# Three of four modulation chunks summed off TensorE, in the opening of a one-core diffusion block

## The chip, the cores and the metric

The kernel is one program on one core of a Trainium2 chip. The metric is device time in microseconds (us). A core has TensorE (PE: matmuls; weight loads are listed as PEld), VectorE (DVE), ScalarE (ACT), GpSimd (POOL) and SyncE (SP, whose queue issues almost all DMAs). They run side by side and wait for each other on semaphores. A matmul writes PSUM, which has eight banks of 512 fp32 columns; everything else lies in SBUF.

## The reference

One layer of a transformer block over 512 latent tokens and 256 context tokens of width 1024, in fp32. What matters here is how it begins:

```
mod_lat = silu(c) @ w_ada + b_ada          # w_ada: 1024 x 6144; shift, scale, gate, twice
mod_ctx = silu(c_ctx) @ w_ada + b_ada
h  = rmsnorm(x,   norm1_g) * (1 + sc1)  + sh1      # latent tokens
hc = rmsnorm(ctx, norm1_g) * (1 + csc1) + csh1     # context tokens
p  = h @ w_in                                       # all columns
pc = hc @ w_in[:, :288]                             # the keys' columns alone
```

Behind it come the latent attention, a short convolution, a gated merge, a gated MLP and the final norm. They hold nine tenths of the time and are not touched.

## The kernel before

Every fp32 matrix product is done as three matmuls: each operand is split into a rounded high part and the low rest, and `mm3` (L420 to L424) adds hi*hi, lo*hi and hi*lo in PSUM. So each weight tile and each activation tile needs two element-wise steps: a copy that rounds (usually ACT) and a subtraction for the low part (DVE or POOL).

The opening makes `h` transposed, feature tile by feature tile (eight tiles `k` of 128 features), and multiplies each with its rows of `w_in` as it comes. Feature tiles are handled in four chunks `c_` of two. For tile k it needs shift and scale, which are columns of `mod_lat` and `mod_ctx`. Of `w_ada` only the 2 x 1024 columns for `sh1` and `sc1` are read here. A chunk is 256 columns of each, times 1024 rows, and comes as four slots of `adaraw` (`ada_load`, L474), each with two row blocks of 128 x 512.

The chunks are summed over the 1024 rows in two ways:

- Chunk 0. For the tokens, DVE accumulates `adaraw * silu(c)` over eight row blocks into PSUM bank 3 and at the end into `first_x` (`first_token`, L1101). For the context, ACT scales the same eight blocks into `parts` (`context_scale`, L788), and POOL adds the eight (`first_context_add`, L611). What is left is a sum over 128 partitions: PE multiplies with a column of ones (`first_sums` L1589; for the context the last four matmuls of `late_columns` L1606), and the result stands as columns, one element per partition. DVE adds the bias (`first_mods` L1132, `first_mods_context` L1140).
- Chunks 1 to 3. The weights are split (ACT `ada_hi` L760, DVE `ada_lo` L1162, one 128 x 1024 tile per slot). PE multiplies them with `chl`, which holds silu(c) and silu(c_ctx) in two parts, 16 matmuls for a chunk (`mod_sums`, L1576), tokens and context at once. ACT copies the four rows out of PSUM (`mod_rows1`, L764), PE turns them into columns (`mod_columns`, L1621), DVE adds the bias (`mods1`, L1166).

With shift and scale for tile k there, ACT computes the high part of `h` (`stream_hi` L778), DVE the value and the low part (`stream_value` L1176, `stream_lo` L1186). PE then does `latents(k)` (L1628): 15 matmuls of 512 columns with the tile of `w_in` that ACT and POOL have split (`latent_hi` L770, `latent_lo` L604). The same helpers with n = 8 to 15 make the context's tiles `chi` and `clo`, after all four chunks.

Before this, four tiles of x are loaded, squared (`token_rms` L745), transposed on PE (`token_columns` L1554) and scaled by their inverse rms, which PE spreads over partitions (`spread_rinv` L1599), ACT copies (`rinv_copy` L755) and DVE applies (`scale_low`, `scale_up`). Two tiles of ctx follow in chunks 1 and 2 (`token_norm` L1155, `lower_copy` L1150, `upper_copy` L740).

After the chunks, PE projects the rotary key (24 matmuls of 512 columns, L1673 to L1678). Then comes the context loop (72 matmuls of 256 columns, L1683 to L1694), which first waits for `cq_lo`: DVE's low part of the query latent (L1246), which stands in DVE's program behind all eight context tiles. The queries and keys follow.

The order of work on each engine is the order in which its block is written. DVE's opening is L1194 to L1242, ACT's L793 to L850, POOL's L618 to L628, PE's L1641 to L1694, SP's L497 to L514. An `ada_load` of the first twelve waits, for its slot, until the earlier user has read it.

Of the kernel before, what the change touches and what calls it, by code (L numbers as in the profile page):

```python
# [26 lines left out]
P = 128  # L27
D = 1024
T = 512
# [42 lines left out]
U_KR = U_ADA + 2 * DT - 4  # L72
# [25 lines left out]
def build(nc, x, c, ctx, c_ctx, w_ada, b_ada, norm1_g, w_in, q_norm_g, kv_norm_g, w_uq, w_ukv, conv_w,  # L98
# [3 lines left out]
    with stack:  # L102
# [8 lines left out]
        whi = sb("whi", [P, SLOTS, UNIT], F32R)  # L111
        wlo = sb("wlo", [P, SLOTS, UNIT], F32R)
# [29 lines left out]
        sb("gap0", [P, 768], scope=early)  # L142
# [148 lines left out]
        def arrived(e, u, slot):  # L291
            r = slot % RAW
            if isinstance(u, int) and u < U_KR:
                e.wait_ge(ada_loaded[slot], 32 * (u // SLOTS + 2))
            else:
                e.wait_ge(raw_loaded[r], 32 * ((u - r - U_KR) // RAW + 1) if isinstance(u, int) else (u - r - U_KR) * 16 + 32)
# [115 lines left out]
        def context_part(k):  # L412

            return parts[:, k, :]
# [36 lines left out]
        def _(sp):  # L451
# [143 lines left out]
        def _(pool):  # L595
# [15 lines left out]
            def first_context_add(k):  # L611

                pool.wait_ge(s("ctx_part"), k + 1)
                wait(pool, s("first_ctx"), k - 1)
                nc.gpsimd.tensor_tensor(out=first_ctx, in0=context_part(0) if k == 1 else first_ctx, in1=context_part(k),
                                        op=ALU.add).then_inc(s("first_ctx"), 1)
# [105 lines left out]
        def _(act):  # L722
# [41 lines left out]
            def mod_rows1(c_):  # L764

                used(act, 4 * c_ - 1)
                wait(act, s("cols1_ps"), c_ + 1)
# [10 lines left out]
            def stream_hi(n):  # L778
# [3 lines left out]
                if n >= DT and k < 2:  # L782
                    act.wait_ge(s("mods1_ctx"), 4)
# [4 lines left out]
            def context_scale(k):  # L788

                act.wait_ge(ada_loaded[k // 2], 32)  # L790
                nc.scalar.activation(context_part(k), first_part(k), ACT.Copy, scale=cvec[:, k, 1:2]).then_inc(s("ctx_part"), 1)
# [3 lines left out]
            token_rms(0)  # L795
            rinv_copy(0)
            context_scale(2)
            context_scale(3)
            token_rms(1)
            rinv_copy(1)  # L800
            token_rms(2)
            rinv_copy(2)
            token_rms(3)
            latent_hi(0)
            rinv_copy(3)
            context_scale(4)
            context_scale(5)
            stream_hi(0)
            stream_hi(1)
            context_scale(6)  # L810
            context_scale(7)
            latent_hi(1)
            for c_ in range(1, CHUNKS):
                for u in range(4 * c_ - 4, 4 * c_):
                    ada_hi(u)
                mod_rows1(c_)
# [278 lines left out]
        def _(dve):  # L1095
# [5 lines left out]
            def first_token(k):  # L1101

                dve.wait_ge(ada_loaded[k // 2], 32)
                if k == 0:
                    nc.vector.tensor_scalar(ps[:, 3, :], first_part(k), cvec[:, k, 0:1], None, ALU.mult).then_inc(s("first_x"), 1)
                else:
                    dve.wait_ge(s("first_x"), k)
# [32 lines left out]
            def first_mods_context():  # L1140

                dve.wait_ge(s("prm_ps"), 2)
                for j in range(2):
                    at = CTX_SUM_AT + j
                    nc.vector.tensor_scalar(shift[:, 1:2, j], ps[:, 7, at:at + 1], prm[:, R_BADA + j:R_BADA + j + 1], None,
                                            ALU.add).then_inc(s("mods1_ctx"), 1)
                    nc.vector.tensor_scalar(gain[:, 1:2, j], ps[:, 7, at + 2:at + 3], prm[:, R_N1 + j:R_N1 + j + 1],
                                            gain0[:, j:j + 1], ALU.mult, ALU.add).then_inc(s("mods1_ctx"), 1)
# [13 lines left out]
            def ada_lo(u):  # L1162

                split_lo(dve, u, u % SLOTS, nc.vector)
# [10 lines left out]

            def stream_value(n):  # L1176
# [3 lines left out]
                if n >= DT and k < 2:  # L1180
                    dve.wait_ge(s("mods1_ctx"), 4)
# [4 lines left out]
            def stream_lo(n):  # L1186
# [37 lines left out]
            for c_ in range(1, CHUNKS):  # L1224
                for u in range(4 * c_ - 4, 4 * c_):
                    ada_lo(u)
                if c_ == 2:
# [3 lines left out]
                    first_mods_context()  # L1231
                mods1(c_)
# [308 lines left out]
        def _(pe):  # L1541
# [34 lines left out]
            def mod_sums(u):  # L1576

                c_, n = u // 4 + 1, u % 4
                unit(u)
                if n == 0:  # L1580
                    wait(pe, s("rows1"), c_ - 1)
                    pe.wait_ge(s("mods1"), 4 * c_)
# [6 lines left out]
            def first_sums(j):  # L1589
# [7 lines left out]
                last.then_inc(s("cols1_ps"), 1)  # L1597

# [22 lines left out]
            def mod_columns(c_):  # L1621

                pe.wait_ge(s("rows1"), c_)
# [431 lines left out]
```

## Time and profile before

| what | value |
|---|---|
| three timed runs | 840.03, 840.4, 841.66 us; median 840.4 |
| the profiled execution | 841.12 us, of it a span of 839.1 us |
| PE busy | 811.4 us (97% of the span) |
| DVE, ACT, POOL busy | 467.1, 373.6, 381.2 us |
| TensorE's granted clock, mean | 0.989 of full speed |

Times below are microseconds from the start of the span. A row of the timeline gives the start, the busy time, the engine, the line, the operation, output and inputs, how many instructions were merged, and in brackets how long the engine had been idle and what ended that. Matmuls overlap: one of 512 columns is listed with 0.39 us although the next one starts 0.23 us later.

### The profile page before, as it was taken

How to read it: one execution, taken by the hardware profiler on the slowest of the kernel's cores; microseconds unless marked ns; L12 is line 12 of the kernel's file. 1: busy time of each engine (PE TensorE's matmuls, PEld its weight loads, DVE VectorE, ACT ScalarE, POOL GpSimd, SP SyncE). 2: the span in 40 equal slices, each digit the busy share in tenths (PEclk: the TensorE clock that was granted, in tenths of full speed). 3: DMA queues.
4: the chain of work that ended last, by engine and by line, in shares of the span. 5: the costliest groups of instructions: out<-in, count | busy, mean ns of one | idle time of the engine just before them, and what ended most of it. 6: DMA issues, size and time to landing. Idle time of an engine off the chain costs nothing.

```text
span 839.1 us, 11438 instructions
## 1 busy us (share of the span) xinstructions
PE 811.4 (97%) x3937; PEld 676.4 (81%) x3937; DVE 467.1 (56%) x635; ACT 373.6 (45%) x592; POOL 381.2 (45%) x197
## 2 busy tenths in 40 slices
PE   4799999999999999999999999999999999999996
PEld 4578977888888888888788988888888888888884
DVE  4787596788888467877303565555555555000005
ACT  6566456666667322322423664334444433221125
POOL 2623494436442554555544054444444444443434
PEclk9899999999999999999899999999999999999998
DMA  8661242111110688777273033333333332322212
GB/s 288 208 193 48 54 113 64 33 44 52 26 51 27 212 261 267 237 231 221 78 249 101 1 101 116 87 97 100 100 100 100 91 93 92 100 101 100 85 42 101
DMA packets 120289, 97.82 MB, mean 117 GB/s; under 512 B 13660, under 2 KB 106105, under 8 KB 120249
## 3 DMA queue, kind: packets, MB, share of 16 engines
q1 hardware_dynamic: 120137, 97.26, 37.9%
q8 instruction: 25, 0.41, 0.2%
q14 instruction: 15, 0.12, 0.1%
q10 hardware_dynamic: 112, 0.04, 0.0%
HBM read 95.17 MB, written 2.10 MB: 116 GB/s over the span
## 4 chain that ended last, share of the span: by engine, by line
PE 89%; DVE 5%; ACT 3%; POOL 1%; issue 1%; DMA 1%; SPq 0%; POOLq 0%; DVEq 0%; ACTq 0%
PE ps L422 25%; PE ps L424 24%; PE ps L423 24%; PE ps L1725 7%; PE ps L1832 3%; PE ps L1821 2%; DVE wlo L341 1%; PE ps L1585 1%; DMA adaraw<-w_ada_dram 1%; POOL wlo L341 1%; ACT work L749 1%; PE ps L1899 0%; PE ps L1917 0%; DVE x L1520 0%; ACT work L1073 0%
## 5 line engine op out<-in xcount | busy, mean ns | idle before, releaser
L341 POOL TENSOR_TENSOR wlo<-raw,whi 128x1024 fp32r<-128x1024 f32 (+4 forms) x125 | 281.2, 2257 | 363.7 <-ACT whi L333 363.2
L422 PE MATMUL ps<-hhi,whi 128*128 128x512 f32 (+1 forms) x520 | 196.2, 377 | 0.2 <-DVE hlo L1467 0.2
L424 PE MATMUL ps<-hhi,wlo 128*128 128x512 f32 (+1 forms) x520 | 195.8, 377 | 0.0
L423 PE MATMUL ps<-hlo,whi 128*128 128x512 f32 (+1 forms) x520 | 195.7, 376 | 0.0
L333 ACT ACTIVATE whi<-raw 128x1024 fp32r<-128x1024 f32 (+4 forms) x125 | 118.2, 957 | 132.4 <-PE ps L424 77.5
L424 PEld LDWEIGHTS ps<-hhi,wlo 128*128 128x128 f32 x520 | 97.9, 188 | 18.1
L422 PEld LDWEIGHTS ps<-hhi,whi 128*128 128x128 f32 x520 | 97.9, 188 | 18.1 <-DVE hlo L1467 0.4
L423 PEld LDWEIGHTS ps<-hlo,whi 128*128 128x128 f32 x520 | 97.9, 188 | 17.8
L1495 DVE SCALAR_TENSOR_TENSOR work<-ps,prm,work 128x511 f32<-128x511 f32 x44 | 33.0, 750 | 75.0 <-ACT work L1049 74.0
L1400 DVE SCALAR_TENSOR_TENSOR adacc<-ada,cvec,adacc 128x1024 f32<-128x1024 f32 x28 | 60.7, 2204 | 18.5 <-DMA ada<-w_ada_dram 18.4
L422 PE MATMUL ps<-whi,fhi 128*128 128x512 f32 x176 | 69.8, 396 | 0.0
L423 PE MATMUL ps<-wlo,fhi 128*128 128x512 f32 x176 | 69.7, 396 | 0.0
L424 PE MATMUL ps<-whi,flo 128*128 128x512 f32 x176 | 69.7, 396 | 0.0
L1049 ACT ACTIVATE work<-ps,prm 128x512 f32<-128x512 f32 x44 | 34.2, 778 | 72.2 <-PE ps L424 72.1
L1518 DVE TENSOR_TENSOR ps<-ps,gbc 128x512 f32<-128x512 f32 x8 | 5.5, 688 | 102.9 <-PE ps L424 102.9
L1504 DVE TENSOR_TENSOR work<-work 128x512 f32<-128x512 f32 x22 | 44.2, 2010 | 6.2 <-DVE work L1498 3.8
L1725 PE MATMUL ps<-hhi,whi 128*128 128x512 f32 x96 | 38.8, 404 | 2.1 <-POOL wlo L341 2.1
L1346 DVE TENSOR_REDUCE ps<-ps 128x1 f32<-128x768 f32 x32 | 30.9, 965 | 17.0 <-PE ps L424 16.7
L422 PEld LDWEIGHTS ps<-whi,fhi 128*128 128x128 f32 x176 | 33.1, 188 | 8.3 <-DVE work L1498 0.4
L424 PEld LDWEIGHTS ps<-whi,flo 128*128 128x128 f32 x176 | 33.1, 188 | 8.0
L423 PEld LDWEIGHTS ps<-wlo,fhi 128*128 128x128 f32 x176 | 33.1, 188 | 7.9
L1056 ACT ACTIVATE fhi<-work 128x512 f32 (+1 forms) x22 | 13.9, 633 | 57.1 <-DVE work L1504 57.1
(290 smaller groups left out, 1533.2 us busy)
## 6 DMA issues: line engine op xcount, KB each, us to landing
raw<-w_up_dram SPq DMA_DIRECT2D x88, 256.0 KB, 3.2
ada<-w_ada_dram SPq DMA_DIRECT2D x32, 512.0 KB, 6.3
raw<-w_in_dram SPq DMA_DIRECT2D x56, 256.0 KB, 4.3
raw<-w_down_dram SPq DMA_DIRECT2D x44, 256.0 KB, 2.7
adaraw<-w_ada_dram SPq DMA_DIRECT2D x32, 256.0 KB, 4.8
raw<-w_o_dram SPq DMA_DIRECT2D x16, 256.0 KB, 3.1
xt<-x_dram SPq DMA_DIRECT2D x4, 512.0 KB, 7.3
raw<-w_attn_out_dram SPq DMA_DIRECT2D x8, 256.0 KB, 2.8
```

What stands on the lines that cost most here:

```text
L333: ins = nc.scalar.activation(h, r, ACT.Copy)
L341: ins = (engine or nc.gpsimd).tensor_tensor(out=l, in0=r, in1=h.bitcast(F32), op=ALU.subtract)
L422: pe.matmul(o, l[0], r[0], start=start, stop=False)
L423: pe.matmul(o, l[0], r[1], start=False, stop=False)
L424: return pe.matmul(o, l[1], r[0], start=False, stop=stop)
L1049: nc.scalar.activation(work[:, 3 * jj + n, :], ps[:, (4 if first else 0) + 2 * jj + n, :], ACT.Identity, bias=col(prm, R_FB + n * FT + j), ...
L1346: nc.vector.reduce_max(top, wide(2 * (turn(g) % 2)), AX.X, negate=True).then_inc(s("nmax"), 1)
L1400: nc.vector.scalar_tensor_tensor(out=adacc[:, gg:gg + D], in0=ada2[:, n % 3, :], scalar=cvec[:, k, 0:1], in1=adacc[:, gg:gg + D], op0=ALU. ...
L1495: nc.vector.scalar_tensor_tensor(out=u[:, 1:T], in0=p[:, 0:T - 1], scalar=col(prm, R_FW + n * FT + j), in1=u[:, 1:T], op0=ALU.mult, op1=AL ...
L1504: nc.vector.tensor_tensor(out=work[:, 3 * jj + 2, :], in0=work[:, 3 * jj, :], in1=work[:, 3 * jj + 1, :], op=ALU.mult).then_inc(s("f_prod" ...
L1725: last = pe.matmul(ps[:, 7, :], tile_of(wlo if term == 2 else whi, u % SLOTS, k), (hlo if term == 1 else hhi)[:, k, :], start=i == 0, stop ...
L1832: last = pe.matmul(ps[:, 6, q], vs[:, kt, h, :], p_[:, kt, q], start=kt == 0 and n == 0, stop=kt == KT - 1 and n == 1)
```

## The change

Chunks 1 and 2 are now summed as chunk 0 is; chunk 3 alone still goes through the split weights. So `mod_sums` runs once instead of three times, and `U_KR`, the number of weight units before the rotary key's, goes from 12 to 4.

- DVE does `first_token(k, c_)` for eight blocks in chunks 1 and 2, ACT `context_scale(k, c_)`, POOL `context_add(c_, k)`. Chunk 1's scaled blocks go to `parts1`, which lies where `wlo` lies; chunk 2's reuse `parts`, which lies where `chi` and `clo` lie.
- PE does `vector_sums(c_)` for the tokens in the chunk, and `context_sums()` for both context chunks once, after all eight `latents`. DVE's `mods_context(1)` and `(2)` follow it. All eight context tiles on ACT and DVE, and PE's context loop, now wait for all twelve context values (`mods1_ctx` at 12), where before only the first two tiles waited for four.
- In the token phase ACT scales two context blocks between one x tile's squares and its `rinv_copy`, and copies the last tile's before `latent_hi(0)`. DVE takes `token_rinv(0)` before `first_token(2)`.
- POOL does all seven adds of chunk 0 before `latent_lo(0)`; chunk 1's seven stand behind `latent_lo(3)`, chunk 2's behind `latent_lo(5)`.

```diff
-U_KR = U_ADA + 2 * DT - 4
+U_KR = U_ADA + SLOTS
+VECTOR_CHUNKS = 3
...
@@ SP, ada_load: every slot waits for both readers
-                    if u < SLOTS:
-                        sp.wait_ge(s("first_x"), 2 * u + 2)
-                        sp.wait_ge(s("ctx_part"), 2 * u + 2)
-                    else:
-                        sp.wait_ge(w_lo, u - SLOTS + 1)
+                    sp.wait_ge(s("first_x"), 2 * u + 2)
+                    sp.wait_ge(s("ctx_part"), 2 * u + 2)
...
@@ POOL
-            for k in range(1, 4):
-                first_context_add(k)
+            for k in range(1, DT):
+                context_add(0, k)
             latent_lo(0)
             latent_lo(1)
-            for k in range(4, DT):
-                first_context_add(k)
-            for k in range(2, DT):
-                latent_lo(k)
+            for c_ in (1, 2):
+                latent_lo(2 * c_)
+                latent_lo(2 * c_ + 1)
+                for k in range(1, DT):
+                    context_add(c_, k)
+            latent_lo(DT - 2)
+            latent_lo(DT - 1)
...
@@ ACT
+            for t in range(TT):
+                token_rms(t)
+                if t < TT - 1:
+                    context_scale(2 * t + 2)
+                    context_scale(2 * t + 3)
+                rinv_copy(t)
             latent_hi(0)
-            rinv_copy(3)
-            context_scale(4)
-            context_scale(5)
             stream_hi(0)
             stream_hi(1)
-            context_scale(6)
-            context_scale(7)
             latent_hi(1)
             for c_ in range(1, CHUNKS):
-                for u in range(4 * c_ - 4, 4 * c_):
-                    ada_hi(u)
-                mod_rows1(c_)
+                if c_ < VECTOR_CHUNKS:
+                    for k in range(DT):
+                        context_scale(k, c_)
+                else:
+                    for u in range(SLOTS):
+                        ada_hi(u)
+                    mod_rows1()
...
@@ ACT stream_hi and DVE stream_value
-                if n >= DT and k < 2:
-                    act.wait_ge(s("mods1_ctx"), 4)
+                if n >= DT:
+                    act.wait_ge(s("mods1_ctx"), 12)
...
@@ DVE
+            token_rinv(0)
             first_token(2)
             first_token(3)
-            token_rinv(0)
...
             for c_ in range(1, CHUNKS):
-                for u in range(4 * c_ - 4, 4 * c_):
-                    ada_lo(u)
+                if c_ < VECTOR_CHUNKS:
+                    for k in range(DT):
+                        first_token(k, c_)
+                else:
+                    for u in range(SLOTS):
+                        ada_lo(u)
...
+            for c_ in (1, 2):
+                mods_context(c_)
             for n in range(DT, 2 * DT):
                 stream_value(n)
                 stream_lo(n)
...
@@ PE
+            def vector_sums(c_):
+                pe.wait_ge(s("first_x"), DT * (c_ + 1))
+                pe.wait_ge(s("mods1"), 4 * c_)
+                for m in range(4):
+                    last = pe.matmul(ps[:, 3, m:m + 1], first_x[:, m * P:(m + 1) * P], ones[:, 0:1], start=True, stop=True)
+                last.then_inc(s("cols1_ps"), 1)
+
+            def context_sums():
+                pe.wait_ge(s("first_ctx"), VECTOR_CHUNKS * (DT - 1))
+                pe.wait_ge(s("xT_low"), KT)
+                for c_ in (1, 2):
+                    for m in range(4):
+                        last = pe.matmul(ps[:, 5, 4 * c_ + m:4 * c_ + m + 1], context_sum(c_)[:, m * P:(m + 1) * P], ones[:, 0:1],
+                                         start=True, stop=True)
+                last.then_inc(s("prm_ps"), 1)
...
                 if c_ + 1 < CHUNKS:
-                    for u in range(4 * c_, 4 * c_ + 4):
-                        mod_sums(u)
-                    latents(2 * c_ + 1, (0,) if c_ else (2,))
-                    mod_columns(c_ + 1)
-                    latents(2 * c_ + 1, (1, 2, 3, 4) if c_ else (3, 4))
+                    if c_ + 1 < VECTOR_CHUNKS:
+                        vector_sums(c_ + 1)
+                        latents(2 * c_ + 1, every if c_ else (2, 3, 4))
+                    else:
+                        for u in range(SLOTS):
+                            mod_sums(u)
+                        latents(2 * c_ + 1, (0,))
+                        mod_columns()
+                        latents(2 * c_ + 1, (1, 2, 3, 4))
...
             pe.wait_ge(s("mods1"), 2 * DT)
+            context_sums()
             for n in range(2):
                 u = U_KR + n
                 unit(u)
...
             pe.wait_ge(s("cq_lo"), 1)
+            pe.wait_ge(s("mods1_ctx"), 12)
             for k in range(DT):
```

## Rows read from the trace of the kernel before

**Rows 1.** The page: busy time, share of the span, instructions of each engine.

```profile
PE 811.4 (97%) x3937; PEld 676.4 (81%) x3937; DVE 467.1 (56%) x635; ACT 373.6 (45%) x592; POOL 381.2 (45%) x197
```

**Rows 2.** Waits between 20 and 80 us: total, times, longest.

```profile
PE ps L1585 <- DVE wlo L341: 2.7, 3, 1.0
```

**Rows 3.** Timeline of the token phase: first_token (DVE), rinv_copy (ACT).

```profile
9.05 1.61 DVE L1108 SCALAR_TENSOR_TENSOR ps<-adaraw,cvec,ps 128x512 f32<-128x512 f32 x2 [1.69 <-DMA adaraw<-w_ada_dram]
...
14.59 1.61 DVE L1108 SCALAR_TENSOR_TENSOR ps<-adaraw,cvec,ps 128x512 f32<-128x512 f32 x2
...
11.62 0.28 ACT L758 ACTIVATE work<-ps 128x128 f32<-128x128 f32 x1 [2.50 <-PE ps L1603]
```

**Rows 4.** Timeline of PE, from the first latents to the context loop.

```profile
23.88 0.77 PE L422 MATMUL ps<-hhi,lqhi 128*128 128x512 f32 x1 [0.95 <-DVE hlo L1191]
...
46.01 1.05 PE L1618 MATMUL ps<-ones,work 128*128 128x1 f32 x8
...
55.46 1.04 PE L1572 MATMUL ps<-ident,xt 128*128 128x128 f32 x8
...
65.20 0.40 PE L422 MATMUL ps<-hhi,lqhi 128*128 128x512 f32 x1
...
77.57 0.40 PE L424 MATMUL ps<-hhi,lklo 128*128 128x512 f32 x1
...
83.28 0.28 PE L422 MATMUL ps<-chi,lkhi 128*128 128x256 f32 x1
```

**Rows 5.** Timeline of DVE: splits, modulation columns, context tiles, low query part.

```profile
27.81 8.62 DVE L341 TENSOR_TENSOR wlo<-adaraw,whi 128x1024 fp32r<-128x1024 f32 x4 [0.93 <-ACT whi L333]
39.44 0.22 DVE L1171 TENSOR_SCALAR shift<-ps,prm 128x2 f32<-128x2 f32 x1 [3.01 <-PE ps L1625]
...
40.08 1.00 DVE L1183 TENSOR_SCALAR ht<-xnT,gain,shift 128x512 f32<-128x512 f32 x1
...
44.89 4.62 DVE L341 TENSOR_TENSOR wlo<-adaraw,whi 128x1024 fp32r<-128x1024 f32 x4
...
59.48 4.63 DVE L341 TENSOR_TENSOR wlo<-adaraw,whi 128x1024 fp32r<-128x1024 f32 x4
...
75.51 0.77 DVE L1191 TENSOR_TENSOR clo<-ht,chi 128x256 fp32r<-128x256 f32 x1 [1.90 <-ACT chi L785]
...
81.70 1.40 DVE L1246 SCALAR_TENSOR_TENSOR cqlo<-ps,prm,cqhi 128x512 fp32r<-128x512 f32 x2
```

**Rows 6.** Timeline of POOL: adds of context parts.

```profile
12.58 2.68 POOL L615 TENSOR_TENSOR work<-work,parts 128x512 f32<-128x512 f32 x2 [3.89 <-ACT parts L791]
...
28.58 8.99 POOL L615 TENSOR_TENSOR work<-work,parts 128x512 f32<-128x512 f32 x4
```

**Rows 7.** Groups by shape, 0 to 100 us: busy, mean ns, idle before.

```profile
L608 POOL TENSOR_TENSOR lqlo<-raw,lqhi 128x384 fp32r<-128x384 f32 x8 | 8.6, 1081 | 0.0
```

**Rows 8.** Timeline of ACT: context parts, square of a ctx tile, first context tiles.

```profile
24.80 1.32 ACT L791 ACTIVATE parts<-adaraw,cvec 128x512 f32<-128x512 f32 x2
...
57.03 1.05 ACT L749 ACTIVATE work<-xt 128x1024 f32<-128x1024 f32 x1
...
74.82 2.07 ACT L785 ACTIVATE chi<-xnT,shift,gain 128x256 fp32r<-128x256 f32 x4
```

**Rows 9.** Windows: from:to, length, busy (instructions) per engine, granted clock, DMA share, GB/s.

```profile
22.00:22.50 0.50, 0.36 (x3) 0.36 (x3) 0.46 (x2) 0.50 (x2) 0.41 (x1) 0.92 0.00 0
...
24.00:28.00 4.00, 4.00 (x10) 3.13 (x11) 2.67 (x6) 3.92 (x7) 1.09 (x2) 0.50 0.43 137
...
29.00:29.50 0.50, 0.50 (x3) 0.36 (x3) 0.50 (x1) 0.50 (x1) 0.50 (x1) 0.75 0.87 231
...
112.00:116.00 4.00, 1.91 (x9) 1.26 (x8) 3.84 (x6) 3.31 (x6) 3.86 (x3) 1.00 0.43 89
...
832.00:835.00 3.00, 0.00 (x0) 0.00 (x0) 2.76 (x5) 1.85 (x6) 3.00 (x2) 0.97 0.04 14
```

More of the change, by code:

```diff
@@ L410, in first_part, with context_part, context_sum @@
             return adaraw[:, k // 2, k % 2 * T:(k % 2 + 1) * T]
-        def context_part(k):
-            return parts[:, k, :]
+        def context_part(c_, k):
+            return (parts1 if c_ == 1 else parts)[:, k, :]
+        def context_sum(c_):
+            return (first_ctx, ctx1[:], parts[:, 0, :])[c_]
         def tile_of(t, slot, k, n=P):
@@ L609, in latent_lo, with context_add @@
                 ins.then_inc(s("win_lo"), 1)
[L611 to L616, printed above, removed]
-            for k in range(1, 4):
-                first_context_add(k)
+            def context_add(c_, k):
+                pool.wait_ge(s("ctx_part"), DT * c_ + k + 1)
+                wait(pool, s("first_ctx"), (DT - 1) * c_ + k - 1)
+                nc.gpsimd.tensor_tensor(out=context_sum(c_), in0=context_part(c_, 0) if k == 1 else context_sum(c_),
+                                        in1=context_part(c_, k), op=ALU.add).then_inc(s("first_ctx"), 1)
+            for k in range(1, DT):
+                context_add(0, k)
             latent_lo(0)
             latent_lo(1)
-            for k in range(4, DT):
-                first_context_add(k)
-            for k in range(2, DT):
-                latent_lo(k)
+            for c_ in (1, 2):
[5 more added lines that the diff above has]
+            latent_lo(DT - 1)
             pool.wait_ge(w_lo, U_KR)
@@ L762, in ada_hi, with mod_rows1 @@
                 split_hi(act, u, u % SLOTS)
-            def mod_rows1(c_):
-                used(act, 4 * c_ - 1)
-                wait(act, s("cols1_ps"), c_ + 1)
+            def mod_rows1():
+                used(act, SLOTS - 1)
+                act.wait_ge(s("cols1_ps"), CHUNKS)
                 nc.scalar.activation(rows1[:], ps[0:4, 3, :], ACT.Copy).then_inc(s("rows1"), 1)
@@ L1174, in mods1, with vector_mods @@
                                             gain0[:, k:k + 1], ALU.mult, ALU.add).then_inc(s("mods1"), 1)
+            def vector_mods(c_):
+                dve.wait_ge(s("cols1_ps"), c_ + 2)
+                for j in range(2):
+                    k = 2 * c_ + j
+                    nc.vector.tensor_scalar(shift[:, 0:1, k], ps[:, 3, j:j + 1], prm[:, R_BADA + k:R_BADA + k + 1], None,
+                                            ALU.add).then_inc(s("mods1"), 1)
+                    nc.vector.tensor_scalar(gain[:, 0:1, k], ps[:, 3, 2 + j:3 + j], prm[:, R_N1 + k:R_N1 + k + 1],
+                                            gain0[:, k:k + 1], ALU.mult, ALU.add).then_inc(s("mods1"), 1)
             def stream_value(n):
@@ L1179, in stream_value @@
                 dve.wait_ge(s("mods1"), 2 * k + 2)
-                if n >= DT and k < 2:
-                    dve.wait_ge(s("mods1_ctx"), 4)
+                if n >= DT:
+                    dve.wait_ge(s("mods1_ctx"), 12)
                 dve.wait_ge(s("xT_low" if k < 4 else "xT_up"), TT if n < DT else KT)
@@ L1576, in mod_sums @@
             def mod_sums(u):
-                c_, n = u // 4 + 1, u % 4
+                n = u
                 unit(u)
                 if n == 0:
-                    wait(pe, s("rows1"), c_ - 1)
-                    pe.wait_ge(s("mods1"), 4 * c_)
+                    pe.wait_ge(s("mods1"), 4 * VECTOR_CHUNKS)
                 for i in range(2):
@@ L1619, in late_columns, with mod_columns @@
                 last.then_inc(s("prm_ps"), 1)
-            def mod_columns(c_):
-                pe.wait_ge(s("rows1"), c_)
+            def mod_columns():
+                pe.wait_ge(s("rows1"), 1)
                 for m in range(4):
```

53 lines of the change are left out of this document (28 added, 25 removed).

## The prediction, on record before the changed kernel ran

> **What bounds the kernel now.** I read the page first: PE is busy 811.4 us of 839.1 [rows 1], so the whole is PE-bound and only a stretch where PE waits can give time without removing matmuls. The waits of the opening come next. From 20 to 80 us PE waited for DVE's weight splits three times, 2.7 us in all [rows 2]. The other cost of the sums through weights is PE's own work. Then the timelines, engine by engine, because the change rewrites four programs and each of its waits has to be placed. Three times matter on PE: the latents start at 23.88, the last `mod_sums` is over at 65.20, the last latents at 77.81 (77.57 + 0.24); and the context loop starts at 83.28 [rows 4]. What follows the context loop is untouched and hangs on it: ACT's and DVE's statistics read the loop's banks, and they feed the queries. So I price the change by how far the loop's start moves.
>
> **What is taken from PE.** 32 of 48 `mod_sums` matmuls. A matmul of 512 columns comes every 0.23 us (24 from 77.81 to 83.28 [rows 4]): 32 x 0.23 = 7.4 us. `vector_sums` costs what `mod_columns` did, about 1.0 us (the four column sums of `late_columns` take 1.05 [rows 4]). `context_sums` adds eight, 2.0 us. PE's own work falls by 5.4 us. Whether that arrives depends on the waits, and I now walk through them.
>
> **Token phase: 1.6 us earlier.** `token_rinv(0)` stood behind two `first_token` that waited 1.69 for a DMA until 9.05 and ran 1.61; so ACT sat idle 2.50 until 11.62 [rows 3]. Now the first inverse is ready near 9.3, and ACT fills the gap with two context parts (1.32 a pair [rows 8]). Tile 1's squares start near 10.7 instead of 13.0; from there the x tiles' DMAs and the alternation of the engines take part of it back. I take 1.6 for the first latents, 23.88 to 22.3; below, 0.5 (DMA-bound); above, 2.3.
>
> **Chunk 1.** DVE was free for it at 26.9 (27.81 less 0.93 [rows 5]), now at 25.3. Two dependent `first_token` take 1.61, so one each 0.86 [rows 3]; eight take 6.9, to 32.2. ACT's eight parts (0.61 each) and the loads, which now follow earlier readers, are done before. PE has 21 matmuls in hand, 7.4 us as before (half of them at half clock), until 29.7, and waits 2.5. Sums 1.0, columns on DVE 0.64 (39.44 to 40.08 [rows 5]): 33.9, against 40.1. Here the change is 6 us ahead.
>
> **Chunk 2.** From the columns' arrival to the next chunk DVE took 5.45 (39.44 to 44.89 [rows 5]); 0.45 of it was a 1.00 us `stream_value` that met POOL, and POOL's `latent_lo(2)` is now over by then. So 33.2 + 5.0 = 38.2, plus 6.9 = 45.1. PE meanwhile: nine matmuls, 15 of `latents(2)`, 1.5 of `late_columns`: done at 40.5. Then it stands at `vector_sums(2)` for 4.6 us, although `latents(3)`, written behind it, is ready at 37. The sums end at 46.1.
>
> **Chunk 3.** `latents(3)` takes 3.5 at full clock, until 49.6. But the clock fell at 22.4 after three microseconds with little on PE, and rose again at 29.2 [rows 9]; at half clock ten matmuls took 4.0 us where ten take 2.3. Under load that lasted 5.3 us (23.88 to 29.2), 13 matmuls with 0.18 more each. After a silence of 4.6 I expect a fall, and these 2.4 more: 52.0. ACT and DVE then need the ctx tile: from PE's transposes (55.46 [rows 4]) to ACT's squares (57.03 [rows 8]) to the first split (59.48 [rows 5]) it took 4.0. Splits start at 53.6, or 56.0 with the fall.
> Beside them runs POOL. One add alone takes 1.34, and 2.25 beside DVE's splits, which then take 2.15 instead of 1.15 (8.62 for four against 4.63) [rows 5, 6]. `latent_lo(3)` ends near 37.1 (1.08 for its larger half [rows 7], 1.7 for both), chunk 1's adds at 46.5, `latent_lo(4)` and `(5)`, which wait for their high parts, at 50.9, and chunk 2's seven would end at 60.3 alone. From 53.6 all four splits meet adds: 8.6, to 62.2. From 56.0 three do: 3 x 2.15 + 1.15 = 7.6, to 63.6. The last four `mod_sums` end 1.1 later: 63.3, or 64.7 with the fall, against 65.20. So nearly all of the six microseconds is given back: the removed matmuls had stood where the others now wait.
> [...]
>
> **The end: 5.3 us later.** From the last `mod_sums` PE is solid: 12.6 us to the end of the latents (65.20 to 77.81). That puts it at 75.9 to 77.3. Before, the context tiles were made while PE was in the last latents (ACT from 74.82 [rows 8]), and `cqlo` began at 81.70 [rows 5], in time for 83.28. Now nothing of the context starts until: `context_sums` 2.0; eight columns on DVE 1.3 and a handover 0.15; ACT's first tile 0.6 (of 2.07 for four); DVE's eight tiles 6.0 (75.51 to 81.70 was 6.2 with one slow); `cqlo` 0.75. Sum 10.8 after the latents, where the loop started after 5.5. The rotary key's matmuls hide 5.5 of it; 3.4 is a new PE silence. If DVE's part overlapped perfectly with the sums the least is 9.5; with POOL's splits in the way 11.8.
>
> **Sum.** Loop start 75.9 + 10.8 = 86.7 without a fall in chunk 3, 77.3 + 10.8 = 88.1 with it: +3.4 or +4.8. After the 3.4 us silence a second fall may slow the loop's 72 matmuls: nothing to 2.4; a silent gap of 2.1 at 112 to 116 left the clock at 1.00, and the silence at the end of the kernel shows the fall between 832 and 835 [rows 9]. I take half, 1.2. Forecast +6.0: 847.1 for an execution like the profiled one (841.12: span 839.1 and 2.0 around it), and 846.4 against the median of 840.4.
>
> **The rivals.**
> A, no fall of the clock: +3.4, 843.8. For it: the gap of 2.1 without one. Against it: 4.6 is more than double.
> B, more loss: both falls in full and one more in the 2.5 us wait of chunk 1, or a DMA behind one of the new waits (an `ada_load` now waits for ACT's and DVE's reading): +8 to +9, 849.
> C, faster: the splits of chunk 3 run alone, 4.6 instead of 8.6. It decides at one point, whether POOL has finished chunk 2's adds when DVE starts to split (53.6 without a fall). Then `mod_sums` ends at 59.3, latents at 71.9, loop at 82.7; with `first_token` at its busy 0.75 instead of 0.86, 1.8 less again: -2.4, 838.0. Against it: 21 adds and six latent pairs are 38 us of POOL even alone, and chunk 1's start only after `latent_lo(3)`.
> D, no change: the token phase gives 2.3, the splits meet two adds and not four, and no fall: 3.4 - 0.7 - 2.0 = +0.7, 841.1.
>
> **How the numbers follow.** Forecast 0.50, A 0.22, B 0.12, D 0.08, C 0.08. The range 842.3 to 849.6 leaves out C, D and the far edge of B. A difference under 0.2% (1.7 us) can't be told from none: slower 0.85, same 0.08, faster 0.07.
>
> **What would show it.** PE's first latents near 22.3; PE idle before `vector_sums(1)` by 2.5 and before `vector_sums(2)` by 4 to 5, with a granted clock of half behind it; four splits of DVE in 7 to 9 us beside POOL's adds; the last latents ending 0.5 to 2 earlier than 77.81; then an idle PE before the context loop, with `cqlo` as what ends it, and the loop near 87 to 88. I am wrong if the loop starts before 84, if PE doesn't wait there, or if the time behind the loop doesn't shift with it.

## The result: 850.6 us, slower by 1.1%

| what | before | after |
|---|---|---|
| median of the timed runs | 840.4 us (838.87 to 841.66, 5 runs) | 850.61 us (850.01 to 850.98, 5 runs) |
| the profiled execution, its span | 841.12, 839.1 | 850.98, 849.2 |
| context loop starts | 83.28 | 92.46 |
| mean granted clock | 0.989 | 0.977 |

The ratio is 1.0114 [1.0103, 1.0125]. The forecast was 846.4, its range 842.3 to 849.6: the direction was right, the size fell a microsecond outside the range. 9.2 us of the loss stand at the start of the context loop, the rest behind it. The page after, busy time of each engine:

```profile
PE 811.5 (96%) x3921; PEld 676.1 (80%) x3921; DVE 475.9 (56%) x651; ACT 374.4 (44%) x598; POOL 399.2 (47%) x211
```

PE is as busy as before [rows 1], although 32 matmuls of `mod_sums` are gone: the eight of `context_sums` are new, and more of the rest run at half clock and take longer (mean granted clock 0.977, before 0.989). The waits of PE between 20 and 110 us (who waited <- for what, us in total, times, longest):

```profile
PE ps L1632 <- DVE work L1116: 7.3, 2, 3.7
PE ps L431 <- DVE clo L1211: 3.7, 1, 3.7
PE ps L1613 <- DVE wlo L346: 3.5, 4, 1.8
```

Before there were three waits on `wlo`, 2.7 us in all [rows 2]. Now the two column sums wait 7.3, the context loop 3.7, and the one chunk of splits that is left 3.5, more than the three did. PE's timeline after, in the same columns as [rows 4]:

```profile
22.74 0.77 PE L431 MATMUL ps<-hhi,lqhi 128*128 128x512 f32 x1 [1.17 <-DVE hlo L1211]
...
32.90 1.86 PE L1632 MATMUL ps<-ones,work 128*128 128x1 f32 x8 [3.63 <-DVE work L1116]
34.62 0.77 PE L431 MATMUL ps<-hhi,lqhi 128*128 128x512 f32 x1
...
47.71 1.86 PE L1632 MATMUL ps<-ones,work 128*128 128x1 f32 x8 [3.69 <-DVE work L1116]
49.43 0.77 PE L431 MATMUL ps<-hhi,lqhi 128*128 128x512 f32 x1
...
54.68 1.03 PE L1601 MATMUL ps<-ident,xt 128*128 128x128 f32 x8
...
68.47 0.40 PE L1613 MATMUL ps<-wlo,chl 128*128 128x512 f32 x1
...
81.30 0.95 PE L1641 MATMUL ps<-ones,ctx 128*128 128x1 f32 x8
82.11 1.03 PE L1641 MATMUL ps<-ones,parts 128*128 128x1 f32 x8
...
92.46 0.36 PE L431 MATMUL ps<-chi,lkhi 128*128 128x256 f32 x1 [3.71 <-DVE clo L1211]
```

Both groups of column sums come after a silence of 3.6 to 3.7 us and take 1.86 where four sums took 1.05 before [rows 4]. The granted clock in those stretches (stretch, length, PE busy, PEclk, DMA share, GB/s):

```profile
26.00:29.00 3.00, 3.00 (x14) 1.00 0.54 152
33.00:36.00 3.00, 3.00 (x11) 0.50 0.99 313
36.00:39.00 3.00, 3.00 (x8) 0.50 0.60 204
48.00:50.00 2.00, 2.00 (x9) 0.50 0.90 304
50.00:53.00 3.00, 3.00 (x9) 0.50 0.66 197
64.00:66.00 2.00, 1.80 (x4) 0.50 0.01 4
108.00:109.00 1.00, 1.00 (x4) 0.50 0.89 236
```

0.50 is 1.2 GHz, 1.00 is 2.4 GHz. Between 26 and 110 us the clock is down four times: from the end of each wait for the column sums into the matmuls behind them, in the middle of the last splits, and once behind the loop. DVE's timeline after shows how its stages went:

```profile
26.51 2.47 DVE L1116 SCALAR_TENSOR_TENSOR ps<-adaraw,cvec,ps 128x512 f32<-128x512 f32 x3
...
32.10 0.75 DVE L1116 SCALAR_TENSOR_TENSOR work<-adaraw,cvec,ps 128x512 f32<-128x512 f32 x1
34.80 0.22 DVE L1191 TENSOR_SCALAR shift<-ps,prm 128x1 f32<-128x1 f32 x1 [1.96 <-PE ps L1632]
35.43 0.54 DVE L1203 TENSOR_SCALAR ht<-xnT,gain,shift 128x512 f32<-128x512 f32 x1
36.76 1.10 DVE L1203 TENSOR_SCALAR ht<-xnT,gain,shift 128x512 f32<-128x512 f32 x1
37.90 1.38 DVE L1211 TENSOR_TENSOR hlo<-ht,hhi 128x512 fp32r<-128x512 f32 x1
39.39 1.59 DVE L1168 TENSOR_SCALAR xt<-xt,small 128x1024 f32<-128x1024 f32 x1
40.91 0.74 DVE L1113 TENSOR_SCALAR ps<-adaraw,cvec 128x512 f32<-128x512 f32 x1
41.75 5.05 DVE L1116 SCALAR_TENSOR_TENSOR ps<-adaraw,cvec,ps 128x512 f32<-128x512 f32 x6
...
57.95 0.77 DVE L1168 TENSOR_SCALAR xt<-xt,small 128x1024 f32<-128x1024 f32 x1
58.77 8.84 DVE L346 TENSOR_TENSOR wlo<-adaraw,whi 128x1024 fp32r<-128x1024 f32 x4
```

And POOL's:

```profile
38.70 1.74 POOL L621 TENSOR_TENSOR ctx<-parts 128x512 f32<-128x512 f32 x1
40.58 8.61 POOL L621 TENSOR_TENSOR ctx<-ctx,parts 128x512 f32<-128x512 f32 x6
...
53.55 10.75 POOL L621 TENSOR_TENSOR parts<-parts 128x512 f32<-128x512 f32 x6
64.80 1.72 POOL L621 TENSOR_TENSOR parts<-parts 128x512 f32<-128x512 f32 x1 [0.50 <-POOL parts L621]
```

The four splits begin at 58.77 and take 8.84, to 67.61; the adds run until 66.52, so that each split meets them. `mod_sums` ends at 68.70, where before it was 65.20.

### The profile page after: what moved, and what is told of

It is laid out like the page before. It is cut to its first block, busy times and chain, and to the rows that moved or that the text cites. A ratio compares the mean times of both kernels' runs of the same rounds, so it can differ in the third digit from the quotient of the medians.

```text
span 849.2 us, 11477 instructions
## 1 busy us (share of the span) xinstructions
PE 811.5 (96%) x3921; PEld 676.1 (80%) x3921; DVE 475.9 (56%) x651; ACT 374.4 (44%) x598; POOL 399.2 (47%) x211
## 4 chain that ended last, share of the span: by engine, by line
PE 83%; DVE 2%; ACT 2%; issue 2%; POOL 1%; DMA 1%; POOLq 0%; SPq 0%; ACTq 0%; DVEq 0%
PE ps L431 23%; PE ps L433 23%; PE ps L432 23%; PE ps L1777 7%; PE ps L1884 3%; PE ps L1873 2%; DMA raw<-w_ukv_dram 1%; PE ps L1951 0%; PE ps L1969 0%; DVE x L1549 0%; ACT work L1080 0%; PE ps L1920 0%; DVE ps L1547 0%; ACT whi L338 0%; ACT chi L794 0%
## 5 line engine op out<-in xcount | busy, mean ns | idle before, releaser
L1429 DVE SCALAR_TENSOR_TENSOR adacc<-ada,cvec,adacc 128x1024 f32<-128x1024 f32 x28 | 65.5, 2381 | 13.3 <-DMA ada<-w_ada_dram 13.3
L1777 PE MATMUL ps<-hlo,whi 128*128 128x512 f32 x96 | 38.5, 401 | 0.0
```

The source lines that it names most:

```text
L1429: nc.vector.scalar_tensor_tensor(out=adacc[:, gg:gg + D], in0=ada2[:, n % 3, :], scalar=cvec[:, k, 0:1], in1=adacc[:, gg:gg + D], op0=ALU. ...
L1777: last = pe.matmul(ps[:, 7, :], tile_of(wlo if term == 2 else whi, u % SLOTS, k), (hlo if term == 1 else hhi)[:, k, :], start=i == 0, stop ...
```

## The experiments

There were seventeen runs, each beside runs of the kernel before. Its medians in the five sets were 842.06, 841.8, 841.45, 841.62 and 841.69. Some kernels issue matmuls that nothing needs, into a bank that is free there, to keep PE busy; four (adds_short, short_filled, short_filled_early and short_early) leave out chunk 2's context sum but for 8 of its 512 columns. "Loop" is the start of the context loop in the profile.

| kernel | us | ratio to before [95%] | loop |
|---|---|---|---|
| tail_alone | 847.38 | 1.0069 [1.0047, 1.0091] | 87.50 |
| tail_filled | 844.51 | 1.0036 [1.0023, 1.0049] | 87.58 |
| ctx_early | 845.38 | 1.0045 [1.0031, 1.0059] | 88.86 |
| adds_short | 846.17 | 1.0060 [1.0039, 1.0080] | 88.13 |
| adds_later | 846.54 | 1.0062 [1.0040, 1.0084] | 89.35 |
| token_alone | 835.29 | 0.9933 [0.9907, 0.9958] | 78.19 |
| token_again | 835.30 | 0.9919 [0.9904, 0.9934] | 79.08 |
| token_warm | 836.52 | 0.9927 [0.9899, 0.9955] | 79.01 |
| after_again | 852.04 | 1.0127 [1.0095, 1.0159] | 92.30 |
| latents_first | 848.67 | 1.0084 [1.0052, 1.0116] | 88.24 |
| filler | 850.90 | 1.0107 [1.0075, 1.0139] | 92.56 |
| both_filled | 847.21 | 1.0072 [1.0049, 1.0095] | 89.41 |
| early_and_first | 845.84 | 1.0042 [1.0021, 1.0063] | 89.24 |
| all_filled | 842.42 | 1.0002 [0.9988, 1.0016] | 84.62 |
| short_filled | 842.61 | 1.0006 [0.9997, 1.0016] | 85.08 |
| short_filled_early | 841.68 | 0.9999 [0.9990, 1.0009] | 83.85 |
| short_early | 838.84 | 0.9959 [0.9945, 0.9973] | 81.25 |

**The tail.** The kernel before, with nothing of the change but the context's sums and tiles behind the last latents; and the changed kernel with the sums ahead of `latents(7)`.

```diff
 # tail_alone, on the kernel before: late_columns no longer sums first_ctx
+            context_sums()          # PE: its four columns, behind latents(7)
 ...
-                    first_mods_context()
+            first_mods_context()    # DVE: behind all latent tiles
 # ctx_early, on the changed kernel
                 else:
+                    context_sums()
                     latents(2 * c_ + 1, every)
```

> The kernel before, with one thing of the change: the four column sums of the context's chunk 0, and the eight context tiles that need them, come only behind the last latents, instead of beside the second chunk. Tail theory (the new wait of the context loop is a serial chain): sums 1.0, four columns on DVE 0.75, then 7.85 as in the changed kernel from its last column (84.6) to the loop (92.46), 9.6 behind the last latents instead of 5.5, so the loop starts 4.1 later at 87.4 and the whole takes 844.5. Rival (the context tiles are hidden by the rotary key's matmuls and the loss sits in the chunks): within 1 us of the kernel before, 840.4 to 841.4. Rival (clock: a silence of over 3 us on PE lets the clock fall in the loop): 2 more, 846.5.

> The changed kernel, with the eight column sums of the context placed before the last latents instead of behind them; nothing else. Tail theory: the sums end at 79.7 instead of 83.1, the chain of 9.3 behind them is the same, so the loop starts at 89.1 instead of 92.5 and the whole is 3.4 shorter, 847.2. Rival (the loop is held by something else than this chain, the rotary key's matmuls or POOL's splits): under 1 us shorter, 849.6 to 850.6.

The loop started where it was expected both times: 87.50 in tail_alone and 88.86 in ctx_early. The tail by itself costs 4.2 us at the loop; the early sums give back 3.6 of it in the changed kernel. The wholes missed in both directions. ctx_early came out 1.8 under its 847.2, with executions spread from 843.36 to 848.83; the profiled one is the slowest of the ten. tail_alone came out 2.9 over its 844.5; the kernel before was 1.7 higher in this set too, and the rest shows behind the loop's start in its profile: from there to the queries it took 10.1 (87.50 to 97.6) where the kernel before took 8.5. tail_filled puts 13 matmuls that nothing needs into that wait.

```diff
 # tail_filled, on tail_alone, ahead of PE's context loop
+            filler(13)
             pe.wait_ge(s("cq_lo"), 1)
```

> The kernel before with only the context's sums and tiles moved behind the last latents, and 13 matmuls that nothing needs in the wait ahead of the context's loop. Theory (of the 6 us that the moved tail costs, 4.2 are its length and the rest is the clock that falls in the wait of 3.1 us ahead of the loop): loop start again 87.5, block from there to the queries 8.5 us instead of 10.1, the whole 845.8, 1.6 less than without the fillers. Rival (the clock falls by the thin column sums and conditions earlier in the tail and not by that wait): 847.4 as without them.

The granted clock behind the loop's start, tail_alone first:

```profile
88.00:92.00 4.00, 4.00 (x25) 0.62 0.02 4
```

```profile
88.00:92.00 4.00, 4.00 (x36) 1.00 0.02 4
```

Loop at 87.58, 8.6 to the queries, and 2.9 us less on the whole (844.51; 2.3 less when each is taken against its own runs of the kernel before). So the wait of 3.1 us in front of the loop costs its own length and, through the clock, 1.5 in the loop and some 2 on the whole.

**The adds beside the splits.** adds_short does chunk 2's seven adds on 8 of 512 columns; adds_later does them in full, but behind the splits.

```diff
 # adds_short
-                nc.gpsimd.tensor_tensor(out=context_sum(c_), ...)
+                n = 8 if c_ == 2 else T
+                nc.gpsimd.tensor_tensor(out=context_sum(c_)[:, 0:n], ...)
 # adds_later: POOL behind latent_lo(5)
+            pool.wait_ge(w_lo, U_KR)
+            for k in range(1, 4):
+                context_add(2, k)
             latent_lo(DT - 2)
             latent_lo(DT - 1)
+            for k in range(4, DT):
+                context_add(2, k)
```

> The changed kernel, with POOL's seven adds of chunk 2 cut from 512 to 8 columns each, so that the sum of the context's chunk 2 is left out of the result in all but 8 columns. Contention theory: DVE's four splits, 8.84 us beside the adds, run alone in 4.65; mod_sums ends 4.2 earlier, and since PE is solid from there to the last latents all of it arrives: 846.4. Rival (the splits are slow for another reason, or POOL's order behind them sets the end): under 1 us shorter, 849.6 to 850.6.

> The changed kernel with all of GpSimd's adds, but chunk 2's seven put behind the last weight splits: three ahead of latent_lo(6), four behind latent_lo(7). Theory (the adds cost only by standing beside the splits): the splits begin at 58.7 as in the changed kernel, take 4.6 us instead of 8.8, the last mod_sums end near 64.5, the loop starts near 88.1, the whole 846 to 847, as with the adds left out. Rival (the adds only move their cost: latent_lo(6) and (7) or the rotary key's splits are late for TensorE): the last latents end at 79 or later, loop start 90 or more, the whole 848 to 850.

DVE, POOL and the first of PE's context sums in adds_later:

```profile
57.89 0.75 DVE L1173 TENSOR_SCALAR xt<-xt,small 128x1024 f32<-128x1024 f32 x1
58.72 4.63 DVE L346 TENSOR_TENSOR wlo<-adaraw,whi 128x1024 fp32r<-128x1024 f32 x4
```

```profile
63.42 4.13 POOL L621 TENSOR_TENSOR parts<-parts 128x512 f32<-128x512 f32 x3 [10.54 <-DVE wlo L346]
...
73.89 4.13 POOL L621 TENSOR_TENSOR parts<-parts 128x512 f32<-128x512 f32 x3 [0.50 <-POOL parts L621]
```

```profile
78.13 1.02 PE L1646 MATMUL ps<-ones,ctx 128*128 128x1 f32 x8 [0.94 <-issue]
```

The splits begin at 58.72, as in the changed kernel (58.77), and take 4.63 instead of 8.84; adds_short shows the same (58.65, 4.63). Both wholes are 4 us below the changed kernel (4.4 and 4.1). The rival showed in a small part only: the loop was at 89.35 and not at 88.1, since POOL's last adds ended at 78.02 and PE, whose context sums need them, began these 0.9 late. The adds cost by where they stand.

**The order and the clock in the chunks.** latents_first puts what is ready (`latents(1)`, `latents(3)`) ahead of the next chunk's column sums, so that PE's silence comes later and is shorter. after_again is the changed kernel itself. filler puts 12 matmuls that nothing needs ahead of each column sum, both_filled 14 and 23 of them, and 15 ahead of the loop.

```diff
 # latents_first
-                        vector_sums(c_ + 1)
-                        latents(2 * c_ + 1, every if c_ else (2, 3, 4))
+                        if c_:
+                            latents(3, every)
+                        vector_sums(c_ + 1)      # latents(1) whole, ahead of it
 # both_filled (filler: 12 and 12)
             def vector_sums(c_):
+                filler(14 if c_ == 1 else 23)
 ...
+            filler(15)
             pe.wait_ge(s("cq_lo"), 1)
```

> The changed kernel, with PE's order changed alone: it does the rest of latents(1) before vector_sums(1), and latents(3) before vector_sums(2), instead of standing at the sums with that work ready. Order theory (PE's in-order wait for DVE's eight first_token holds back the ctx tile's transposes, and by them ACT's squares and the splits of chunk 3): splits begin near 53.7 instead of 58.8, the loop starts at 87.4 and the whole is 5.1 shorter, 845.5. Rival (the splits still meet all adds and the tail is a chain behind DVE, so that nothing passes): under 1 shorter, 849.6 to 850.6.

> The changed kernel itself, beside the others of this job, for the comparison: 1.010 to 1.013 of the kernel before, loop near 92.5.

> The changed kernel, with twelve more matmuls of 512 columns on PE ahead of each vector_sums, into an unused PSUM bank: work that nothing needs, in the wait. Clock theory (the two silences of 3.7 us let the granted clock fall to half, which doubles the column sums from 1.0 to 1.86 twice and slows latents(3) by 1.8): with PE kept at work the clock stays at full, the splits of chunk 3 begin 3.5 earlier and the whole is 3.5 shorter, 847.1, in spite of 5.6 us more of matmuls. Rival (the waits are DVE's alone and the clock costs nothing): same time, 850.6, or longer.

> The changed kernel with matmuls that nothing needs in the three silences of TensorE: 14 in the wait ahead of chunk 2's column sums, 23 in the wait ahead of chunk 3's, 15 in the wait ahead of the context's loop. Theory (the stages lose time at half clock after each silence, and the context tail's own length does the rest): both groups of column sums take 1.05 us instead of 1.86, latents(3) runs in 4.3 instead of 5.25, the last splits begin near 55.3 instead of 58.8, the loop starts near 89 (-3.5), the first context block runs 8.5 instead of 8.55 to 10, the whole 846. Rival (VectorE and not the clock sets the stages; the fillers only load TensorE): splits begin at 58 or later, loop start 92 or more, the whole 850.5 to 852.

latents_first began its splits at 54.41, and they met all the adds (8.98): the loop moved to 88.24, 4.2 earlier (87.4 expected). The whole was 3 above its expectation, with the clock at 0.50 from 88 to 92, inside the loop. filler missed. Its second set of matmuls ended at 44.3; the clock fell in the 2.72 us of silence that were left, and `latents(3)` ran at half clock again; the loop stood at 92.56. both_filled covered the second wait too. Its column sums and the clock in `latents(3)`:

```profile
32.53 0.95 PE L1639 MATMUL ps<-ones,work 128*128 128x1 f32 x8
...
46.45 1.05 PE L1639 MATMUL ps<-ones,work 128*128 128x1 f32 x8 [0.16 <-DVE work L1116]
```

```profile
48.00:50.00 2.00, 2.00 (x10) 1.00 0.77 259
50.00:53.00 3.00, 3.00 (x19) 1.00 0.44 120
```

Full clock, sums of 0.95 and 1.05, loop 89.41 (3.05 earlier, 3.5 expected; the splits began at 55.79, and during them the clock fell as in the changed kernel). The rival, that the clock costs the stages nothing, is out: of the 9.2 us at the loop the falls behind the two waits are worth 3.05. But one execution isn't the next. PE's column sums in after_again:

```profile
32.68 1.05 PE L1632 MATMUL ps<-ones,work 128*128 128x1 f32 x8 [2.61 <-DVE work L1116]
...
46.69 1.87 PE L1632 MATMUL ps<-ones,work 128*128 128x1 f32 x8 [4.34 <-DVE work L1116]
```

The first came at full clock, only the second at half, and the splits began 1.2 earlier (57.59). That gain was gone before the loop: all four groups of `mod_sums` but the first ran at half clock (0.50 from 62 to 68), the last ended at 68.46 (68.70 in the changed kernel), and the loop started at 92.30. In the loop the clock fell once more (0.58 from 92 to 96).

**Together.** early_and_first joins ctx_early and latents_first; all_filled adds matmuls that nothing needs to it (9 ahead of `latents(2)`, 6 ahead of `latents(4)`, 4 in each unit of `mod_sums`).

> The changed kernel with both orders of PE changed: latents before vector_sums, and the context's column sums before the last latents. If the two costs are separate they add: 5.1 and 3.6, the loop near 83.8 and the whole at 842. Rival (they are one chain, and taking one away leaves the other): no better than the better of the two, 845.

> The changed kernel with the context sums where the kernel before has them, all of latents(1) and latents(3) ahead of the next chunk's column sums, and matmuls that nothing needs: 9 ahead of latents(2), 6 ahead of latents(4), 4 in each unit of the mod_sums. Theory (without the half clock of 36-40, 50-53 and 64-74 that the version without them showed, 1 + 1 + 4 us come back): loop start near 83.5, the whole 840. Rival 1 (the units of mod_sums go at the pace of ScalarE's and GpSimd's adds, so the clock of TensorE there is worth nothing): loop start 87 to 89, the whole 844 to 846. Rival 2 (the fillers lengthen the units): over 846.

early_and_first missed by 4 us: alone, its two edits had given 3.6 and 4.2, together 3.2 (loop 89.24). Its clock:

```profile
60.00:64.00 4.00, 1.94 (x7) 0.98 0.00 0
64.00:68.00 4.00, 4.00 (x14) 0.50 0.01 2
68.00:72.00 4.00, 4.00 (x10) 0.50 0.21 53
72.00:76.00 4.00, 4.00 (x19) 0.74 0.19 49
```

PE was 1.94 busy of 4 between 60 and 64, with four matmuls for each split of 2.2 us. The clock fell there and stayed at half until 74, though PE was solid from 65 on. all_filled kept it up from 52 to 84 (1.00; from 48 to 52 it was 0.58) and started its loop at 84.62: 4.6 of the expected 5.7, at 842.4, level with the kernel before.

What was then open is whether the prices add up, and whether the removed matmuls show at all. short_filled takes away the clock's falls and chunk 2's adds, short_filled_early the late sums as well, short_early is the same without the 15 matmuls ahead of the loop.

```diff
 # short_filled = both_filled + adds_short
 # short_filled_early = short_filled + ctx_early
 # short_early = short_filled_early, less
-            filler(15)
             pe.wait_ge(s("cq_lo"), 1)
```

> The changed kernel with the matmuls that nothing needs in its three silences, and chunk 2's context sum left out but for 8 of its 512 columns. Theory (the prices add up: loop start 92.5 less 3.1 for the clock, as both_filled had it, less 4.2 for the adds): splits begin near 55.8 and take 4.6, loop start near 85.2, the whole 843. Rival (with the splits short the clock falls elsewhere or another wait comes first): loop start 87 or more, the whole 845.

> As short_filled, and the context's sums ahead of latents(7) instead of behind them. Theory (a further 3.6 us, as ctx_early had it): loop start near 81.6, earlier than the 83.28 of the kernel before, the whole 839.5, so that the removed matmuls at last show. Rival (the clock falls between 62 and 75, as it did with the early sums before): loop start 84 or more, the whole 842 or more.

> As short_filled_early, without the 15 matmuls that nothing needs ahead of the context loop. Theory (the three prices add up): the rotary key's matmuls end near 80.4, cq_lo is there, loop start 80.5 to 81.5 against 83.28 of the kernel before, the whole 838.5 to 839. Rival (removed matmuls show nothing, the time behind the loop gives it back): 841 to 842.

short_filled hit (loop 85.08, expected 85.2). short_filled_early missed by my own edit: `cqlo` began at 79.81, but the extra matmuls ran until 84.0 and the loop started at 83.85. Without them the loop started at 81.25 and the whole is 838.84. PE's waits in short_early:

```profile
PE ps L431 <- DVE hlo L1212: 1.2, 1, 1.2
PE ps L1614 <- DVE wlo L346: 0.8, 1, 0.8
PE ps L1625 <- DVE gain L1146: 0.8, 1, 0.8
PE ps L431 <- DVE cqlo L1276: 0.3, 1, 0.3
```

92.46 less 81.25 is 11.2 us for the three causes, against 3.05 (clock) + 4.3 (adds) + 3.6 (sums) = 11.0 measured singly. With all three gone the loop starts 2.0 earlier than before and the whole is 0.4% faster. That does not show that the removed matmuls arrive: 1.1 of the 2.0 us stand at the first latents already (the token phase), chunk 2's context sum is all but left out, and the next three runs have the token phase alone, with all 48 `mod_sums` still on PE, at 835.3, 3.5 below short_early.

**The part that gains.** token_alone is the kernel before with only the token phase's new orders on ACT, DVE and POOL; token_warm adds ten matmuls that nothing needs around the first column sums.

```diff
 # token_alone, on the kernel before
+            for t in range(TT):
+                token_rms(t)
+                if t < TT - 1:
+                    context_scale(2 * t + 2)
+                    context_scale(2 * t + 3)
+                rinv_copy(t)                  # ACT
 ...
+            token_rinv(0)                     # DVE
             first_token(2)
 ...
+            for k in range(1, DT):            # POOL, ahead of latent_lo(0)
+                first_context_add(k)
```

> The kernel before, with the token phase of the change alone: ACT's order (context parts between the squares), token_rinv(0) ahead of first_token(2), and all of POOL's chunk 0 adds before the first latent splits. Two gains by my reading: the first latents 1.1 earlier (22.74 against 23.88 in the changed kernel), and DVE's splits of chunk 1, 8.62 us beside four adds in the kernel before, run alone in 4.65, of which PE's own work hides about a half: 5 us earlier at the second chunk. If both pass to the end: 835.5. Rival (DMA-bound: the slots of chunk 1 come no earlier, so the splits wait for them): 839.3, the 1.1 alone. Rival (PE's work in chunk 1 hides it and later chunks are bound by their own splits): 840.4.

> The kernel before with the changed kernel's token phase alone, as token_alone. Theory: 835.3 again, loop start 78.2. Rival (a lucky clock in the first run): 837 to 838.

> The kernel before with the changed kernel's token phase alone, and ten matmuls that nothing needs (4 ahead of the first column sums, 6 behind them) in TensorE's wait for the first conditions. Theory (the first latents run at half clock after that wait): they start at full clock, end 1.1 us earlier, the last mod_sums end at 59.2 instead of 60.3, the loop starts at 77.1, the whole 834.2. Rival 1 (the conditions or the transposes on VectorE set the pace there, not TensorE): 835.3 as without them. Rival 2 (the ten matmuls push the first sums back): 836 or more.

Twice 835.3, faster than both kernels. DVE and then PE in token_alone:

```profile
25.22 5.09 DVE L341 TENSOR_TENSOR wlo<-adaraw,whi 128x1024 fp32r<-128x1024 f32 x4
```

```profile
78.19 0.28 PE L422 MATMUL ps<-chi,lkhi 128*128 128x256 f32 x1
```

The first latents start 1.6 earlier (22.29), as forecast for the token phase. The rest of the 5.1 us at the loop (4.2 in token_again, where the clock rose later) fits the splits of chunk 1: POOL has ended its adds by then, so the four take 5.09 instead of 8.62 [rows 5]. That is the same contention as in the change, with its sign turned. The changed kernel has no splits in chunk 1 and can't have this part of the gain. Against the token phase alone, the change of the two chunks is a loss of 15 us by the ratios of the first two sets of runs (1.0114 and 0.9933), and of 17.5 by the later ones (1.0127 and 0.9919). token_warm had the clock at 1.00 there and gained nothing: its six last extra matmuls ran from 22.27 to 24.80 and held the first latents until 24.64, so what full clock gave was spent on waiting for them. Rival 2 holds in its time (836 or more), and the matmuls that hold things back are the last six.

## Why the prediction missed, by its own steps

- **Taken from PE: the count right, its worth not shown.** 32 matmuls are gone, but no run separates their 5.4 us from the rest.
- **Token phase: right in kind.** The first latents started at 22.74 (22.3 forecast).
- **Chunk 1: place right, size short by 1.6.** DVE's sums ended at 32.85 (32.2). The fall of the clock that the forecast kept for the 4.6 us wait came in this one of 3.63 too: sums 1.86 and not 1.0, columns on DVE at 34.80 (33.2). In the forecast this fall cost nothing; it was a part of rival B.
- **Chunk 2: the step whose reason failed, 1.1.** "DVE took 5.45 ... 0.45 of it was a 1.00 us `stream_value` that met POOL, and POOL's `latent_lo(2)` is now over by then." It is over, and that `stream_value` took 0.54. But `latent_lo(3)` and chunk 1's adds (38.70 on) take its place. From the columns to the next chunk DVE took 6.11 (34.80 to 40.91) and not 5.0: `xt` alone took 0.84 more (1.59 against the 0.75 of adds_later at 57.89, with POOL idle), and the second `ht` 1.10 where it took 0.96 before. With chunk 1's lateness that is 2.7 us: 40.91 for 38.2. The eight `first_token` themselves took 6.75 (6.9): six of them took 5.05 beside POOL's adds of 40.58 to 49.15, 0.84 each, and three of chunk 1's took 2.47 with POOL idle (26.51), 0.82 each.
- **Chunk 3: fall right, count of the adds wrong by 1.2.** The clock fell; column sums and latents ended at 54.68 (52.0), and the splits began 4.1 behind them (4.0 forecast), at 58.77 (56.0). All four met adds, not three: `mod_sums` ended 9.9 behind the splits' start, at 68.70 (64.7), and not 8.7. The adds had begun 2.65 late and the splits 2.77, so their places to each other were as forecast. What failed is the working: it let the adds end at 60.3 "alone", although each takes 2.25 beside a split. By its own prices 3.2 adds were left at 56.0, and these last until 63.2, past the start of the fourth split.
- **The end: right.** 12.6 to the end of the latents, and from there 11.16 to the loop (10.8 forecast), with the 3.7 us silence (3.4).
- **The second fall:** forecast at 1.2 in the loop's matmuls. Here the loop ran at full clock (8.55 to the queries) and the clock fell at 108; in tail_alone, after_again, latents_first and filler it fell in the loop. Behind the loop's start their profiled executions took 1.8, 0.3, 2.3 and 2.5 us longer than that of the kernel before, the changed kernel's 0.7. That its medians come to 1.0, near the 1.2, is luck: the fall that was priced did not happen in the loop.

So the loop, at 92.46, is 4.4 later than forecast (88.1): 4.0 in the chunk stages (1.6 in chunk 1, 1.1 in chunk 2, 1.2 in chunk 3), 0.4 in the tail; behind the loop it is 1.0, forecast 1.2. The step that failed is the walk through the chunks: it put chunk 1's fall and POOL's adds beside DVE's `xt` at nothing and counted one split too few beside the adds. Rival B (849) named one part of it, a fall in chunk 1's wait, and got a chance of 0.12; DVE's single-input steps beside POOL were in no rival. Rival A is out: neither profiled execution of the changed kernel passed all its waits without a fall, and with the falls behind the three waits covered (both_filled) the whole was still 847.2.

The Trainium skill (SBUF — State Buffer, section Who interferes with whom) says that `tensor_scalar` can enter a mode that takes both ports, and that a VectorE instruction in such a mode contends with GpSimd; only outside these modes is one with at most one SBUF input free of it. The trace agrees as far as the times go; no row shows the mode. `xt`, 128x1024 fp32, takes 0.75 with POOL idle, and beside its adds 1.56 to 1.67 (filler and both_filled), but also 0.77 across the end of one add (57.95 in the changed kernel). How much it loses depends on where it falls.

## What to carry to other kernels

When matmuls are moved off the engine that bounds a kernel, price first what the engine then waits for: a wait of some 3 us cost itself and up to 2 more at half clock here. The prices of such waits added up where the clock was held up (11.0 singly and 11.2 together), and not where it wasn't (3.6 and 4.2 alone, 3.2 together). List for each VectorE step, one-input ones too, what GpSimd does in the same microseconds after the change, not before it. And run the parts of a change singly: here the token phase alone is 6.4 to 6.8 us faster than the kernel before, which the whole change, 10 slower, hides.

## What the runs showed of the hardware that I had not expected

- The clock's falls depend on the execution. In the changed kernel the wait for the first column sums was 3.63 with a fall in one execution (sums 1.86) and 2.61 without one in another (1.05, after_again); in filler the clock fell in a silence of 2.72. From the loop's start to the end a profiled execution took between 756.4 us (early_and_first) and 760.3 (filler), where the instructions are the same: from 92 to 96 the granted clock was 1.00 in the first and 0.50 in the second.
- The clock fell without a long silence, in a stretch where PE was busy 1.94 of 4.00 with gaps of 1.03, and stayed at half for 10 us (63.9 to 74), of which PE was solid for 9 (early_and_first).
- Extra matmuls in front of a wait were worth having only where they covered it nearly to its end (filler left 2.72 of the second wait, both_filled 0.16), and cost their time where the wait was shorter than expected (short_filled_early, 2.8 us).
